# A two-layer block on one core: VectorE adds the last two chunks of squares ahead of three norms' sums

## The reference, cut to what matters

```python
def rmsnorm(x, g):
    xf = x.astype(jnp.float32)
    y = xf * lax.rsqrt(jnp.mean(xf * xf, axis=-1, keepdims=True) + NORM_EPS)
    return (y * g.astype(jnp.float32)).astype(x.dtype)
```

## Time and profile before

| | us |
|---|---|
| timed runs, median (lowest to highest) | 692.96 (692.09 to 694.26) |
| the profiled execution: own time | 692.05 |
| the profiled execution: span | 690.3 |
| PE busy | 650.9 (94%) |
| PEld busy | 541.8 (78%) |
| DVE busy | 338.0 (49%) |
| ACT busy | 326.7 (47%) |
| POOL busy | 379.0 (55%) |

### The profile page before, as it was taken

The page is one execution under the profiler, slowest core; times in us unless marked ns, Lnnn a source line. Parts: engine busy times, 40 slices in busy tenths (PEclk is TensorE's granted clock), DMA queues, the critical chain, the costliest instruction groups (busy, mean ns, idle before and its releaser), DMA issues.

```text
span 690.3 us, 13825 instructions
## 1 busy us (share of the span) xinstructions
PE 650.9 (94%) x5608; PEld 541.8 (78%) x5608; DVE 338.0 (49%) x684; ACT 326.7 (47%) x603; POOL 379.0 (55%) x284
## 2 busy tenths in 40 slices
PE   5999999999999999999999999999999999977894
PEld 4899899999999999998899999999745545533432
DVE  5869823787881247885764555352612211211102
ACT  7566777866554456665357766343311111100104
POOL 3989557798887989999697655784000000000000
PEclk9999999999999999999999999999999999999998
DMA  8875333434447555455356433799999999999993
GB/s 338 328 291 189 122 123 125 182 122 160 146 134 295 187 184 187 176 218 206 128 183 244 130 124 127 308 426 411 361 420 420 424 422 420 421 425 420 420 422 154
DMA packets 27282, 181.59 MB, mean 263 GB/s; under 512 B 3024, under 2 KB 3280, under 8 KB 6864
## 3 DMA queue, kind: packets, MB, share of 16 engines
q1 hardware_dynamic: 26784, 179.61, 66.9%
q10 hardware_dynamic: 432, 1.05, 0.4%
HBM read 179.60 MB, written 1.05 MB: 262 GB/s over the span
## 4 chain that ended last, share of the span: by engine, by line
PE 80%; DMA 10%; DVE 4%; ACT 3%; SPq 1%; issue 1%; POOL 0%; ACTq 0%; DVEq 0%
PE D L523 48%; PE L L1002 7%; DMA wu<-w_expert_dram 4%; DMA ring<-w_expert_dram 4%; PE L L977 3%; PE QB L1050 3%; PE L L706 2%; DMA ring<-w_dense_dram 2%; PE TB L715 2%; PE D L1085 2%; PE D L571 1%; PE TB L1085 1%; PE L L679 1%; SPq L417 1%; DVE small_r L1604 1%; PE D L575 1%
## 5 line engine op out<-in xcount | busy, mean ns | idle before, releaser
L1587 POOL TENSOR_TENSOR ring_r<-ring,ring_r 128x512 fp32r<-128x512 f32 (+1 forms) x280 | 378.8, 1387 | 94.4 <-ACT ring_r L1174 94.1
L523 PE MATMUL D<-scr_r,ring_r 128*128 128x256 f32 x1104 | 209.7, 286 | 0.0
L1174 ACT ACTIVATE ring_r<-ring 128x1024 fp32r<-128x1024 f32 (+2 forms) x140 | 145.2, 1043 | 87.2 <-PE D L523 75.5
L523 PEld LDWEIGHTS D<-scr_r,ring_r 128*128 128x128 f32 x1104 | 172.3, 188 | 2.4 <-issue 1.6
L523 PE MATMUL D<-hT_r,ring_r 128*128 128x256 f32 x552 | 154.2, 279 | 0.0
L523 PE MATMUL D<-big_r,ring_r 128*128 128x256 f32 x1086 | 131.2, 280 | 1.0 <-POOL ring_r L1587 1.0
L523 PEld LDWEIGHTS D<-big_r,ring_r 128*128 128x128 f32 x1086 | 128.4, 188 | 2.7 <-POOL ring_r L1587 1.4
L523 PEld LDWEIGHTS D<-hT_r,ring_r 128*128 128x128 f32 x552 | 103.9, 188 | 1.1 <-issue 0.7
L1604 DVE SCALAR_TENSOR_TENSOR small<-small,L 64x256 f32<-64x256 f32 x16 | 6.6, 412 | 120.7 <-ACT small L1510 120.7
L1510 ACT ACTIVATE small<-L 64x256 f32<-64x256 f32 x16 | 6.0, 378 | 77.6 <-PE L L1002 77.6
L977 PEld LDWEIGHTS L<-wkr,big 128*128 128x128 f32 x240 | 27.9, 191 | 10.6 <-issue 10.6
(11 more groups left out here) (386 smaller groups left out, 1023.3 us busy)
## 6 DMA issues: line engine op xcount, KB each, us to landing
ring<-w_dense_dram SPq DMA_DIRECT2D x69, 1024.0 KB, 4.9
big<-w_expert_dram SPq DMA_DIRECT2D x31, 1024.0 KB, 21.7
ring<-w_expert_dram SPq DMA_DIRECT2D x19, 1024.0 KB, 26.4
spare<-w_expert_dram SPq DMA_DIRECT2D x12, 1024.0 KB, 17.1
ring<-w_expert_dram SPq DMA_DIRECT2D x10, 512.0 KB, 6.8
wu<-w_expert_dram SPq DMA_DIRECT2D x4, 1024.0 KB, 18.6
small<-w_expert_dram SPq DMA_DIRECT2D x4, 1024.0 KB, 17.2
scr<-w_expert_dram SPq DMA_DIRECT2D x4, 1024.0 KB, 18.5
```

The source lines that it names most:

```text
L523: last = mm(out_, r32(w[i][ws]), r32(x[j][xs_]), start=start and m == 0, stop=stop and m == 2)
L1174: A_(r32(hi_unit(j)[w]), dense_unit(j)[w], ACT.Copy).then_inc(hi_ready, 1)
L1587: last = g.tensor_tensor(r32(w), w, r32(h).bitcast(F32), ALU.subtract)
```

## The change: what it does

For N_FIN1, N_ATT2 and N_CQ the last fold now ends with a `step`, and one more VectorE add of 128x256 puts chunk 1 onto chunk 0 and increments the semaphore that TensorE waits for. TensorE then multiplies chunk 0 alone by `ones`. The norm of `c_kv` (two chunks, not folded) and the others stay as they were.

```diff
--- before.py
+++ after.py
@@ -785,9 +785,7 @@
             def sum_folded(n, dst, src):
 
                 pe.wait_ge(folded, n - N_FIN1 + 1)
-                for c in range(2):
-                    last = mm(dst[:, 0:T], ones, src[:, c, :], start=(c == 0), stop=(c == 1))
-                last.then_inc(ssq, 1)
+                mm(dst[:, 0:T], ones, src[:, 0, :], start=True, stop=True).then_inc(ssq, 1)
 
             chunk_pair("cq", x1, "x1")
             pe.wait_ge(lo_of["o"], 8)
@@ -804,9 +802,7 @@
                 chunk("qb", c, h2)
             pe.wait_ge(rooted, N_CQ)
             pe.wait_ge(cq_folded, 1)
-            for c in range(2):
-                last = mm(UB[:, 0:T], ones, cq_sq[:, c, :], start=(c == 0), stop=(c == 1))
-            last.then_inc(ssq, 1)
+            mm(UB[:, 0:T], ones, cq_sq[:, 0, :], start=True, stop=True).then_inc(ssq, 1)
             for c in range(4):
                 chunk("kb", c, h2)
                 if c == 0:
@@ -1837,7 +1833,9 @@
 
                 dve.wait_ge(sq, ready)
                 ins = v.tensor_tensor(src[:, 0:2, :], src[:, 0:2, :], src[:, 2 * i:2 * i + 2, :], ALU.add)
-                ins.then_inc(folded, 1) if i == 3 else step(ins)
+                step(ins)
+                if i == 3:
+                    v.tensor_tensor(src[:, 0, :], src[:, 0, :], src[:, 1, :], ALU.add).then_inc(folded, 1)
 
             for i in range(4):
                 out_end("out1", i)
@@ -1877,7 +1875,8 @@
                 stt(xT[:, c, :], xT[:, c, :], V("final_norm_gain", c), rinv1).then_inc(normed, 1)
             fold(cq_sq, 1, SQ0[N_CQ] + 2)
             dve.wait_ge(sq, SQ0[N_CQ] + 3)
-            v.tensor_tensor(cq_sq[:, 0:2, :], cq_sq[:, 0:2, :], cq_sq[:, 4:6, :], ALU.add).then_inc(cq_folded, 1)
+            step(v.tensor_tensor(cq_sq[:, 0:2, :], cq_sq[:, 0:2, :], cq_sq[:, 4:6, :], ALU.add))
+            v.tensor_tensor(cq_sq[:, 0, :], cq_sq[:, 0, :], cq_sq[:, 1, :], ALU.add).then_inc(cq_folded, 1)
             dve.wait_ge(s_in["wkr_wrt"], 32)
             split("wkr", wkr, wkr_hi, 0, DC)
             dve.wait_ge(s_in["wkr_wrt"], 32)
```

## The result

The change makes the kernel slower: median 696.02 us (694.8 to 700.58, 13 runs) against 692.96 us (691.59 to 694.26, 13 runs), a ratio of 1.004 with a 95% interval of 1.0022 to 1.0059. 695.9 us were forecast. The span of the profiled execution is 694.5 us (before: 690.3).

What follows compares the result with a forecast made beforehand. TensorE's chain of waits (80% of the span) was taken as the bound; 1.86 us for the first two sums plus 1.44 for the third gave 3.3 slower, 695.9 us between 695.35 and 696.26, range 693.2 to 697.4.

Steps and rivals of the forecast that it cites:

- Turns of VectorE and GpSimd: At the folds, VectorE ends 0.28 or 0.55 us after GpSimd's running subtraction; each added add costs 1.43 us of VectorE's time.
- First sum: Sum over scr: add ends at 281.26, TensorE idles 1.12 us and, with the sum 0.43 shorter, is 0.69 us late.
- Second sum: Sum over hT: TensorE idles 1.6 us, loads at 286.15, and is 1.86 us late after both sums.
- VectorE's own lateness is lost in slack: Behind the second sum, VectorE's reciprocal is 2.65 us later, but from 297 us all engines are only 1.86 late.
- Third sum: Sum over cq_sq just covered; the mean and root behind its add come late, costing 1.44 us at line 589.
- The tail: From 444 us on, everything is later by the same 3.3 us, since DMA stretches that are not full move with TensorE.
- otherwise alike: Profile sign: the tail from 444 us on is shifted by 3.3 us and unchanged in other respects.
- The sum: Total of both steps: 1.86 + 1.44 = 3.3 us slower, forecast 695.9 us.
- Quiet adds: Rival: GpSimd gives way at the adds, 0.46 us per add, so 0.35 us slower, about 693; chance 0.10.
- The shorter sums win: Rival: adds end before TensorE reaches the sums and line 589's wait goes unnoticed; 1.3 us faster, 691.7; chance 0.06.
- It doesn't reach the end: Rival: DMA engines, full from 448 us on, take up the shift, so 0.0 us change; chance 0.05.
- further wait: Rival: shifted VectorE turns cause another wait at 300 to 302 us or the next root, 697 to 697.5; chance 0.06.

Runs made afterwards that it cites:

- e4: Whole change, but each last fold writes to PSUM and a reduction from PSUM replaces the add; against the kernel before 0.90 us shorter to 478 us, ratio 0.9977.
- e3: Kernel before with the change's edit for the third norm (cq_sq) alone; the stretch to 478 us is 1.40 us longer.
- e5: Third norm's edit alone, with VectorE's wkr and wrt work moved behind the norm of N_CQ; stretch to 478 us 0.61 us shorter than the kernel before.
- e9: Kernel before plus the three added adds, TensorE still multiplying both chunks; stretch to 478 us 3.36 us longer, one profile.
- e7: Whole change with TensorE's cq chunks 2 and 3 ahead of the first two sums and VectorE's cq_sq, wkr and wrt work reordered; its 1.4 us lead was lost.

## Why the prediction was right, step by step

- **Turns of VectorE and GpSimd.** Right: 0.28 and 0.55 us after the subtraction's end, four times of four in the first fences above, and adds of 1.38 to 1.41 us where 1.43 was taken. e4 shows it from the other side: take the SBUF inputs away and the cost is gone.
- **First sum.** Idle forecast 1.12, measured 1.10.
- **Second sum.** Forecast load at 286.15 and the next chunk 1.86 late; measured 286.17 and 1.88, or 1.81 without this execution's 0.07. The idle ahead of the sum is 1.43, not 1.6. At 299.79 us VectorE's last low halves of hT are 1.88 late (297.91 before), though its reciprocal had been 2.54 late: the step by which VectorE's own lateness is lost in slack held too.
- **Third sum.** The place was right (line 589; e3, e5), the size not quite: 1.44 forecast, 1.09 in the change (2.97 less 1.88) and 1.40 alone in e3. In the change the first fold of cq_sq took 0.68 us instead of 1.05: after an idle of 0.73 us GpSimd's subtraction ran from 306.52 to 307.82, and the fold was issued only as it ended (307.81), where before the fold was issued at 305.91 and had to wait. The 0.37 us of this fold accounts for what is missing; I had taken the timing of VectorE against GpSimd (their phase) as unchanged. The idle of line 589 was forecast at 2.1 and is 1.74 for the same reason.
- **The tail.** Right: the shift at 478 us is the one at line 589, and the windows in which the DMA engines are not full move with it: the dips of the DMA share in 440 to 444 and 492 to 496 us are in 444 to 448 and 496 to 500 us after. These cuts take other parts of the dips. Cut where the shift puts them, the first has a share of 0.33 (442.9 to 446.9 us; 0.32 before), the second 0.37 (496.2 to 500.2, behind the fall of the clock; 0.72 before), and in e9, without that fall, 0.74 (495.3 to 499.3): "otherwise alike" holds but for what the clock does. Windows of after, in the columns of rows 3:

```profile
444.00:448.00 4.00, 4.00 (x37) 4.00 (x36) 1.37 (x2) 2.12 (x2) 4.00 (x4) 1.00 0.16 39
...
496.00:500.00 4.00, 4.00 (x60) 2.55 (x62) 2.52 (x13) 0.00 (x0) 0.00 (x0) 1.00 0.42 122
```

- **The sum.** 3.3 us forecast, 2.91 by the ruler, 3.06 by the medians. That 695.9 lies 0.12 us from the measured 696.02 is partly luck: from the timed runs' own median the sum gives 696.26, and the half-way value took off about what the third sum had too much.
- **The rivals.** Quiet adds were priced at 0.35 us slower; e4, which makes them quiet in fact, is 0.90 faster. The price had the second sum's load at 284.18, as if the quiet adds pushed the folds of hT back, and charged the third add in full; in e4 it loads at 283.97 without idle, since these instructions stand where VectorE waits for a subtraction anyway. "The shorter sums win" needs quiet adds too. "It doesn't reach the end" is out by e9's span (693.7 us against 690.3), and no further wait came at 300 us or at the next root.

The Trainium skill (page "SBUF — State Buffer", section "Who interferes with whom") says that a VectorE instruction with two SBUF inputs contends with a GpSimd instruction that reads SBUF, and that one with at most one SBUF input, outside the 2-port modes, does not. The trace agrees in both directions: the adds with two SBUF inputs wait for GpSimd (1.38 to 1.41 us), and the reduction with its only input in PSUM does not (0.69 us beside a subtraction). The wait doesn't take in the whole record: a held fold ends 0.55 us after the subtraction, where a free one takes 0.69.

## What to carry to other kernels

Price a small VectorE instruction with two SBUF inputs beside a busy GpSimd at a whole turn (here 1.4 us for 0.43 us of work) and add it to everything behind it in the queue, less what VectorE would have waited there anyway. Then look where that queue is awaited; here the third add was paid at the next norm's wait. Saving 0.43 us of TensorE by such an add loses unless the add has no second SBUF input or the queue has room. In e4 folds whose results went to PSUM and were reduced from there cost VectorE only time in which it would have waited.

## What the runs showed of the hardware that was not expected

- Whether a VectorE instruction meets a subtraction shifts with the phase of the two engines: the first fold of cq_sq took 1.05, 0.68 and 1.67 us in before, after and e7 (where it stands ahead of the products for xT), and the four splits 3.31 us before and 4.72 in e7. The change so got back 0.37 us some 28 us behind its first add, and e7 lost the 1.4 us that it had gained.
- The clock at its lower level for 3.4 us near 485 us, in 8 of 14 profiles, worth 1.3 us, as large as most of the effects here.
